# A row of four 512-column matmuls and a row of four 256-column ones, instead of two and two

## The reference

```python
D_MODEL, SEQ = 1024, 256
D_FF = ((8 * D_MODEL // 3 + 127) // 128) * 128        # 2816

def swiglu(h, w_gate, w_up, w_down):
    return (jax.nn.silu(h @ w_gate) * (h @ w_up)) @ w_down

for i in range(DEPTH):                                # DEPTH = 2
    x = x + 0.5 * swiglu(rmsnorm(x, g[i, 0]), ffn_w_gate[i, 0], ffn_w_up[i, 0], ffn_w_down[i, 0])
    x = x + mixer(rmsnorm(x, g[i, 1]))
    x = x + 0.5 * swiglu(rmsnorm(x, g[i, 2]), ffn_w_gate[i, 1], ffn_w_up[i, 1], ffn_w_down[i, 1])
return rmsnorm(x, final_gain)
```

## Time and profile before

| | before |
|---|---|
| median of the runs | 904.14 us (903.95 to 904.39) |
| the profiled execution | 904.11 us |
| its span, first to last instruction | 902.1 us |
| TensorE busy (matmuls) | 874.9 us, 97% |
| TensorE weight loads | 771.1 us, 85% |
| VectorE busy | 634.0 us, 70% |
| ScalarE busy | 470.6 us, 52% |
| DMA queues | 55% of 16 engines |
| mean granted clock of TensorE | 0.992 |

### The profile page before, as it was taken

The page is one execution under the profiler, slowest core; times in us unless marked ns, Lnnn a source line. Parts: engine busy times, 40 slices in busy tenths (PEclk is TensorE's granted clock), DMA queues, the critical chain, the costliest instruction groups (busy, mean ns, idle before and its releaser), DMA issues.

```text
span 902.1 us, 12580 instructions
## 1 busy us (share of the span) xinstructions
PE 874.9 (97%) x5319; PEld 771.1 (85%) x5319; DVE 634.0 (70%) x723; ACT 470.6 (52%) x563; POOL 32.1 (4%) x49
## 2 busy tenths in 40 slices
PE   6999999999999999999999999999997999999996
PEld 5888888889998988888888888888886888888885
DVE  6987776568777697777676787776576687776462
ACT  6755554446555665555454565555445465555442
POOL 1660000000000000000000000000000000000000
PEclk9999999999999999999999999999999999999998
DMA  8776655564444447665556476655655175554611
GB/s 261 225 236 191 195 181 171 182 214 153 141 140 141 141 148 226 187 188 178 186 195 189 138 234 188 188 190 169 209 178 181 52 233 187 187 187 163 195 63 47
DMA packets 152984, 159.18 MB, mean 176 GB/s; under 512 B 2592, under 2 KB 151136, under 8 KB 152928
## 3 DMA queue, kind: packets, MB, share of 16 engines
q1 hardware_dynamic: 152832, 158.35, 55.0%
q10 hardware_dynamic: 96, 0.03, 0.0%
HBM read 157.32 MB, written 1.05 MB: 176 GB/s over the span
## 4 chain that ended last, share of the span: by engine, by line
PE 94%; DVE 2%; ACT 2%; issue 1%; DMA 0%; ACTq 0%; DVEq 0%
PE psum L354 93%; ACT w_hi L648 1%; DVE w_lo L805 1%; PE psum L568 1%; PE psum L554 1%; DMA gains_rows<-in_final_gain_dram 0%; PE psum L462 0%; DVE y_sb L879 0%; DVE x L881 0%; DVE xg L811 0%; DVE y_sb L877 0%; ACT xg L652 0%; DVE x L912 0%; ACT soft L657 0%; ACT scratch L688 0%
## 5 line engine op out<-in xcount | busy, mean ns | idle before, releaser
L354 PE MATMUL psum<-xg,w_hi 128*128 128x512 f32 (+1 forms) x1664 | 490.3, 379 | 5.4 <-issue 2.9
L805 DVE TENSOR_TENSOR w_lo<-raw,w_hi 128x2048 fp32r<-128x2048 f32 x152 | 340.8, 2243 | 123.3 <-ACT w_hi L648 123.3
L354 PEld LDWEIGHTS psum<-xg,w_lo 128*128 128x128 f32 x1536 | 289.0, 188 | 62.5
L648 ACT ACTIVATE w_hi<-raw 128x2048 fp32r<-128x2048 f32 x152 | 283.7, 1867 | 92.7 <-PE psum L354 91.6
L354 PE MATMUL psum<-xg,w_lo 128*128 128x256 f32 x1536 | 312.8, 278 | 0.0
L354 PEld LDWEIGHTS psum<-xg,w_hi 128*128 128x128 f32 x1664 | 254.0, 189 | 9.0 <-issue 7.7
L354 PE MATMUL psum<-h_all,w_hi 128*128 128x512 f32 (+1 forms) x832 | 244.6, 378 | 0.7 <-DVE h_all L1010 0.7
L354 PEld LDWEIGHTS psum<-h_all,w_lo 128*128 128x128 f32 x768 | 144.5, 188 | 31.3
L354 PE MATMUL psum<-h_all,w_lo 128*128 128x256 f32 x768 | 156.4, 278 | 0.0
L354 PEld LDWEIGHTS psum<-h_all,w_hi 128*128 128x128 f32 x832 | 127.0, 189 | 1.5 <-issue 1.5
L678 ACT ACTIVATE scratch<-psum 128x512 f32<-128x512 f32 x44 | 26.2, 595 | 93.7 <-PE psum L354 93.7
(11 more groups left out here) (84 smaller groups left out, 400.4 us busy)
## 6 DMA issues: line engine op xcount, KB each, us to landing
raw<-in_ffn_w_up_dram SPq DMA_DIRECT2D x44, 1024.0 KB, 5.4
raw<-in_ffn_w_gate_dram SPq DMA_DIRECT2D x43, 1024.0 KB, 5.4
raw<-in_ffn_w_down_dram SPq DMA_DIRECT2D x32, 1024.0 KB, 5.2
raw<-in_ffn_w_down_dram SPq DMA_DIRECT2D x16, 768.0 KB, 4.4
raw<-in_attn_w_qkv_dram SPq DMA_DIRECT2D x12, 1024.0 KB, 5.2
raw<-in_attn_w_o_dram SPq DMA_DIRECT2D x4, 1024.0 KB, 4.9
band<-in_x_dram SPq DMA_DIRECT2D x2, 512.0 KB, 4.3
raw<-in_ffn_w_gate_dram SPq DMA_DIRECT2D x4, 256.0 KB, 5.5
```

The costliest lines, as they stand in the source:

```text
L354: return nc.tensor.matmul(out, stationary, moving, start=start, stop=stop, skip_group_check=True)
L648: nc.scalar.activation(w_hi[:, n % SPL, 0:size], raw[:, n % RAW, 0:size], ACT.Copy).then_inc(hi_split, 1)
L805: nc.vector.tensor_tensor(w_lo[:, n % SPL, 0:size], raw[:, n % RAW, 0:size], w_hi[:, n % SPL, 0:size].bitcast(f32), ALU.subtract).then_inc ...
```

## The change

`column_chunks` now takes two chunks k, k + 1 at a time (four terms: two chunks by two banks), and `down` four chunks, or two where a part of six has two left. `split_products` itself stays. So the same matmuls with the same operands come in rows of four 512-column ones and four 256-column ones. The waits within a tile come once for each row of eight, for the later of the chunks.

```diff
-                    for k in ks:
+                    for k in ks[::2]:
                         if j == 0 and side == 0:
-                            pe.wait_ge(xg_lo_done, norm * DC + k + 1)
+                            pe.wait_ge(xg_lo_done, norm * DC + k + 2)
...
-                        last = split_products([(b + m, hi[:, k, m * P:(m + 1) * P], lo[:, k, m * P:(m + 1) * P],
-                                                xg[:, k], k == 0, k == DC - 1) for m in range(GM)])
+                        last = split_products([(b + m, hi[:, i, m * P:(m + 1) * P], lo[:, i, m * P:(m + 1) * P],
+                                                xg[:, i], i == 0, i == DC - 1) for i in (k, k + 1) for m in range(GM)])
+                        k += 1
...
-                            for c0 in range(0, chunks, GM):
-                                k0 = DC * part + c0
+                            for c0 in range(0, chunks, 2 * GM):
+                                c1 = min(c0 + 2 * GM, chunks)
                                 if pair == 0 and e == 0:
-                                    pe.wait_ge(h_lo_done, g0 + k0 // GM + 1)
+                                    pe.wait_ge(h_lo_done, g0 + (DC * part + c1) // GM)
                                 last = split_products([(b, hi[:, c, cols], lo[:, c, cols], h_all[:, DC * part + c],
                                                         DC * part + c == 0, DC * part + c == FC - 1)
-                                                       for c in range(c0, c0 + GM)])
+                                                       for c in range(c0, c1)])
```

## The result

| | before | after |
|---|---|---|
| median of 6 runs each | 903.88 us (902.67 to 904.39) | 908.00 us (907.02 to 908.36) |
| ratio of after to before | | 1.0047, 95% interval 1.0037 to 1.0058 |
| span of the profiled execution | 902.1 us | 906.2 us |

What follows compares the result with a forecast made beforehand. TensorE's stream of matmuls at full clock was taken as the bound: 512 x 10 ns = +5.1 us for the lows, 0 for highs and waits, so 904.11 + 5.1 = 909.2 us; range 903.5 to 911.6, the forecast's own 907.2 to 911.6.

Steps and rivals of the forecast that it cites:

- TensorE's stream as the bound: Whole kernel: TensorE, busy 97% of the span, sets the time by its matmuls' start distances; other engines follow behind.
- 512 merges: FFN gate, up and down: 352 plus 160 times, two groups of two long, two short matmuls become one of four and four.
- Lows, +10 ns a merge: FFN 256-column matmuls: third and fourth of a row take 120 ns instead of 115, +10 ns each time, 512 times.
- Highs, 0 between -6 and +4: FFN 512-column matmuls: third and fourth of a row cost nothing extra, bounded by -6 and +4 ns a merge.
- Coarser waits at nothing: Waits inside FFN tiles, now for two chunks at once: 0 us; 1.2 us were the cover gone.
- a slack of loads that two long matmuls fill: FFN rows: two 512-column matmuls already fill the weight loads' slack, so only the first two 256-column ones go at 115 ns.
- The lower bound for a low: 256-column matmuls in FFN rows: at the 107 ns of attention's transposes, third and fourth would give 16 ns back.
- The rival of no change: FFN rows: load slack carries over, so four and four cost what twice two and two do; 903.3 to 905.5 us, 22%.
- The rival that switches between widths cost: FFN rows: 1,024 fewer width switches save 8 ns on two of each four lows, 8.2 us, giving 895.9 us; 6%.
- The rule of the Trainium skill: TensorE stream: 107 ns a load, 109 a 256-column matmul, so loads are just covered in any order and the sum is 0.

Runs made afterwards that it cites:

- gu_only: Rows of four in the gate and up products alone, down left at rows of two as in the kernel before: 906.59 us, ratio 1.0036 to before.
- eight: Rows of eight 512-column and eight 256-column matmuls (six or four in some places) instead of the change's four: 905.45 us, ratio 1.0026 to the kernel before.
- coarse: The change's coarser waits with the matmuls in the old order of two and two: 903.34 us, ratio 1.0000 to the kernel before.
- one_one: Each 512-column matmul followed at once by its 256-column one, against rows of two in the kernel before: 906.31 us, ratio 1.0033.
- highs31: The change's rows reordered: three 512-column matmuls, two 256-column, one 512-column, two 256-column: 907.06 us, ratio 1.0042 to the kernel before.
- lows13: The change's rows reordered: two 512-column matmuls, one 256-column, two 512-column, three 256-column: 912.76 us, ratio 1.0105 to the kernel before.
- low64_before: The kernel before with FFN low weights of 64 columns instead of 128, half the lo x hi term left out: 909.78 us, ratio 1.0074.
- sixteen: Whole gate and up tiles as sixteen 512-column then sixteen 256-column matmuls, down parts eight or six: 904.04 us, ratio 1.0008 to the kernel before.

## Why the prediction held

909.2 us was forecast, 908.0 measured; slower by 5.1 us was forecast, 4.1 came. The mechanism was right in part: the matmuls' start distances carry the loss, and the third and fourth low of a row are slower than the pairs of before. The reason given for it was wrong, and the sum is as near as it is partly by luck.

- TensorE's stream as the bound, all else behind it: right. The chain, the waits and the other engines' times stayed, and the whole difference stands in the start distances. The loads' records still start with the matmul before, 2 to 5 ns after its start, as the prediction asked.
- 512 merges: right, by `gu_only` in proportion within its interval, in one bank or two.
- Lows, +10 ns a merge between the bounds of -16 and +20: it was +13.2. The third and fourth came at 119, which is +7.3 against a pair of before and not +10. The other +5.9 come from the first two, from 114.6 to 117.1 and from 115.9 to 119.3, and those the prediction had left as they were.
- Highs, 0 between -6 and +4: it was -4.7, most of it from the fourth, at 228.2. The bounds had been taken from pairs; `eight` shows where it leads, to 226.7. The errors of the two terms, +3.2 and -4.7 ns, cancel for the most part. That is luck, and it is why the sum is nearer than its terms.
- Coarser waits at nothing: right, by `coarse`.
- The reason given, a slack of loads that two long matmuls fill, does not hold. By it rows of eight would lose more than rows of four, and rows of one would be no slower than rows of two. `eight` and `one_one` came out the other way, and so a fixed saving for each row is wrong too.
- The lower bound for a low, 107 ns from six transposes in the earlier trace rows: it is a mean of one distance of 168 ns, four of 109 and a last one of 29. In a steady run a transpose takes 109. No term of the sum used it.
- The rival of no change read a quartet as 2 x 228 + 2 x 120, one fixed cost for each matmul. That reading of the bare stream is right, 226.7 and 120; what was wrong is that order would then not matter. Borders add 0 to 26 ns to a cycle of the pattern, and the change went from one of the cheapest, two cycles at 3.4 ns, to one of 15.2 ns.
- The rival that switches between widths cost: wrong here. It needed lows inside a row below 115 ns, and they were at 119. Only from rows of four on do fewer switches help: over the bare stream the kernels with 1,056, 544 and 283 rows lie at 3.6, 7.9 and 5.7 us.
- The rule of the Trainium skill ("TensorE: Matmul & The Clock Gate", section "Back-to-back issue gap"), N by 2.4 plus 2.5 ns, has the slope of the long rows and not their constant: it is 13.3 ns here, for 256 and 512 columns of this type with a load each. The section itself calls the formula the gap of an isolated matmul and says that in a stream the load and the matmul set the spacing together, which the prediction did not say. The earlier trace rows and the earlier trace rows, which it set against the rule, are distances of matmuls and don't measure a load.

Open is what makes the rhythm. The low block of weights takes part, since half its width moves the time by -7.6 us in one pattern and +6.7 in another, but whether by its load or by the output, and where, no run here shows.

## What to carry to other kernels

Where TensorE's stream is the bound and two kinds of matmul alternate, their order is worth some tenths of a per cent, here up to 1%, with not one instruction more or less, and the effect need not grow or fall steadily with the length of the rows. Take a cost for such an order only from a stretch of the trace with that very pattern: costs by place, carried over from another pattern, missed `highs31` and `lows13` by over 5 us, and a cost of the load missed `low64_before` by 10. Only for very long rows did it work: the time of `sixteen` was forecast to 0.7 us.

## What the runs showed of the hardware

- In rows of sixteen the distance of matmuls with a 128-column load each settles at 226.7 ns for 512 columns and 120.0 for 256, after five highs or two lows of the same kind, at a granted clock of 1.00.
- The same instructions ran at 346.7 or 353.3 ns a pair for whole FFNs of one execution (`one_one`), and the switch came at a wait or a boundary. The runs of `one_one` spread from 903.6 to 907.1 us, beside 902.5 to 904.2 for the kernel before.
- Low weight blocks of half the width made rows of two 6.7 us slower and rows of four 7.6 us faster.
